# Six changed orders and three split sums of squares in a two-block layer kernel on one core

## The reference

```python
# block 1
h = rmsnorm(x, norm1_g)
u_a, u_b, u_c, u_d, u_g = split(h @ w_in)
branches = [short_conv(u_a), stick_breaking_attention(u_b), mamba2(u_c), moba(u_d)]
merged = sum(sigmoid(u_g[i]) * (branches[i] @ w_branch[i]))
x = x + merged @ w_o
h2 = rmsnorm(x, norm2_g)
g_ff, up_ff = split(h2 @ w_gate_up)
x = x + (silu(g_ff) * up_ff) @ w_down
x = rmsnorm(x, final_g)
# block 2
h = rmsnorm(x, norm_g_2)
# windowed attention with sinks (q, k, v, za) and a gated token mixing (u, vs, zs)
y = ga * (attention @ w_att_out) + gs * (mixing @ w_sg_out)
out = rmsnorm(x + y @ w_o_2, final_g_2)
```

## Time and profile before

| | us |
|---|---|
| median of 3 runs | 1333.63 (1333.63 to 1334.12) |
| the profiled execution | 1333.23 |
| its span | 1331.20 |
| TensorE busy | 1321.4 |
| VectorE, ScalarE, GpSimd busy | 582.5, 509.6, 597.1 |
| mean granted TensorE clock | 0.998 of full speed |

### The profile page before, as it was taken

One profiled execution on the slowest core, in us unless ns is written; L12 is line 12 of the kernel. 1 busy time (PEld: TensorE's weight loads), 2 busy tenths in 40 slices (PEclk: granted clock), 3 DMA queues, 4 the chain that ended last, 5 costly groups with the idle time before them and its releaser, 6 DMA issues.

```text
span 1331.2 us, 16999 instructions
## 1 busy us (share of the span) xinstructions
PE 1321.4 (99%) x6518; PEld 1081.4 (81%) x6518; DVE 582.5 (44%) x947; ACT 509.6 (38%) x729; POOL 597.1 (45%) x448
## 2 busy tenths in 40 slices
PE   9999999999999999999999999999999999999998
PEld 8877777888888888888888887877777888888887
DVE  3674444556554433213322347766654322242333
ACT  6222534566433533222211236254655224342233
POOL 4453333443644364445554546433432553435441
PEclk9999999999999999999999999999999999999999
DMA  6333152413233343333333323322221332423321
GB/s 202 95 113 102 40 151 64 126 41 119 79 97 134 95 115 106 95 95 95 95 95 95 87 71 111 103 69 77 91 68 59 127 95 64 127 64 100 102 83 64
DMA packets 144493, 126.70 MB, mean 95 GB/s; under 512 B 4464, under 2 KB 139760, under 8 KB 144432
## 3 DMA queue, kind: packets, MB, share of 16 engines
q1 hardware_dynamic: 144080, 125.66, 30.7%
q10 hardware_dynamic: 352, 0.19, 0.1%
HBM read 120.46 MB, written 2.10 MB: 92 GB/s over the span
## 4 chain that ended last, share of the span: by engine, by line
PE 96%; DVE 2%; ACT 1%; issue 0%; DMA 0%; SPq 0%; ACTq 0%; DVEq 0%
PE gemm L592 25%; PE gemm L600 25%; PE gemm L593 25%; PE gemm L649 2%; PE gemm L650 2%; PE gemm L653 2%; PE gemm L616 2%; PE gemm L617 2%; PE gemm L622 2%; PE mix L978 1%; PE mix L966 1%; PE mix L955 1%; PE mix L1032 1%; PE mix L802 1%; PE gemm L677 1%; PE mix L827 0%
## 5 line engine op out<-in xcount | busy, mean ns | idle before, releaser
L525 POOL TENSOR_TENSOR wlo<-raw,whi 128x512 fp32r<-128x512 f32 x424 | 571.9, 1379 | 551.0 <-ACT whi L1130 551.0
L592 PE MATMUL gemm<-hh,whi 128*128 128x512 f32 x1128 | 444.9, 394 | 0.4 <-ACT whi L1130 0.4
L593 PE MATMUL gemm<-hl,whi 128*128 128x512 f32 x1128 | 439.6, 390 | 0.0
L600 PE MATMUL gemm<-hh,wlo 128*128 128x512 f32 x1128 | 280.3, 390 | 0.0
L1130 ACT ACTIVATE whi<-raw 128x2048 fp32r<-128x2048 f32 x106 | 202.5, 1911 | 193.4 <-PE gemm L600 164.6
L592 PEld LDWEIGHTS gemm<-hh,whi 128*128 128x128 f32 x1128 | 211.8, 188 | 49.2 <-issue 4.6
L593 PEld LDWEIGHTS gemm<-hl,whi 128*128 128x128 f32 x1128 | 212.0, 188 | 43.1 <-issue 0.5
L600 PEld LDWEIGHTS gemm<-hh,wlo 128*128 128x128 f32 x1128 | 211.4, 188 | 43.6
L521 POOL TENSOR_TENSOR wlo_b<-raw_b,whi_b 128x512 fp32r<-128x512 f32 x16 | 20.6, 1287 | 146.2 <-ACT whi L1130 146.2
L1850 DVE TENSOR_TENSOR fu_t<-gemm,R 128x512 f32<-128x512 f32 x22 | 15.2, 691 | 99.7 <-PE gemm L600 99.7
L592 PE MATMUL gemm<-ah,whi 128*128 128x512 f32 x132 | 51.5, 390 | 0.5 <-DVE xT L1829 0.5
(11 more groups left out here) (443 smaller groups left out, 1863.9 us busy)
## 6 DMA issues: line engine op xcount, KB each, us to landing
raw<-w_in SPq DMA_DIRECT2D x53, 1024.0 KB, 5.3
raw<-w_gu SPq DMA_DIRECT2D x44, 512.0 KB, 4.7
raw<-w_o SPq DMA_DIRECT2D x8, 1024.0 KB, 5.1
raw<-w_down SPq DMA_DIRECT2D x16, 512.0 KB, 4.0
raw_b<-w_branch SPq DMA_DIRECT2D x16, 256.0 KB, 5.6
raw<-w_ao SPq DMA_DIRECT2D x4, 1024.0 KB, 5.1
raw<-w_so SPq DMA_DIRECT2D x4, 1024.0 KB, 5.0
raw<-w_in SPq DMA_DIRECT2D x7, 512.0 KB, 4.6
```

Source lines behind the costliest of these rows:

```text
L525: last = nc.gpsimd.tensor_tensor(a(wlo), a(raw), as_f32(a(whi)), ALU.subtract)
L592: mm(bank[:, :], w, xh[:, k, :], start=(k == 0), stop=False)
L593: mm(bank[:, :], w, xl[:, k, :], start=False, stop=False)
L600: last = mm(bank[:, :], wlo_[:, s, k, col:col + P], xh[:, k, :], start=False, stop=(k == kts - 1))
```

## The change

Six orders and three sums:

1. In `first_tile`, the 11 fill products behind `turn_in(0)` and `turn_in(1)` become 4, then `turn_in(2)` and `turn_in(3)`, then 5.
2. The sums over partitions of acc0, acc1 and acc2 are no longer one f32 product each. VectorE copies the accumulator to fp32r and subtracts the copy from it; TensorE adds two fp32r products with ones_r. `sum_rows` moves behind the second tile's products of unit 32; `sum_both` moves from unit 66 into the first tile of unit 67, behind ten products.
3. In units 62 to 65, ScalarE's split of the next unit stands between hh and the squares of an odd m instead of ahead of the next hh, and VectorE adds the squares of tile m - 1 in step m (those of 5 and 6 in step 6).
4. `turn_rows` moves into the second tile of unit 67, behind ten products.
5. The split of unit 81 moves ahead of the wait for `ln_var`.
6. `turn_out(0)` moves into unit 104, behind eight products. A seventh, small order on VectorE swaps `finish_q` and a `w_slot` in the attention.

```diff
--- before.py
+++ after.py
@@ -108,6 +108,7 @@
         hh = place("hh", [P, KD, SEQ], 76, f32r)
         hl = place("hl", [P, KD, SEQ], 92, f32r)
         c1 = place("c1", [P, 640], 108)
+        ones_r = place("ones_r", [P, P], 110.5, f32r)
         prm = place("prm", [P, NPAR], 112)
         sml = place("sml", [P, 256], 113)
         R = place("R", [P, SEQ], 114)
@@ -157,6 +158,8 @@
 
         acc0 = place("acc0", [P, SEQ], Z0)
         sq0 = place("sq0", [P, 2, SEQ], Z0 + 2)
+        acc0h = place("acc0h", [P, SEQ], Z0 + 6, f32r)
+        acc0l = place("acc0l", [P, SEQ], Z0 + 8, f32r)
 
         ah = place("ah", [P, 8, SEQ], Z0, f32r)
         al = place("al", [P, 8, SEQ], Z0 + 16, f32r)
@@ -164,6 +167,8 @@
         fu_t = place("fu_t", [P, 2, SEQ], Z0 + 68)
         acc1 = place("acc1", [P, SEQ], Z0 + 32)
         acc2 = place("acc2", [P, SEQ], Z0 + 34)
+        acch = place("acch", [P, 2, SEQ], Z0 + 48, f32r)
+        accl = place("accl", [P, 2, SEQ], Z0 + 52, f32r)
         sq1 = place("sq1", [P, 2, SEQ], Z0 + 36)
         sq2 = place("sq2", [P, 2, SEQ], Z0 + 40)
         r1 = place("r1", [P, SEQ], Z0 + 44)
@@ -681,9 +686,12 @@
                 pe.wait_ge(sem("ident_in"), 16)
                 for m in range(2):
                     turn_in(m)
-                idle_products(11)
+                idle_products(4)
+                for m in range(2, 4):
+                    turn_in(m)
+                idle_products(5)
                 for k in range(KD):
-                    if k in (0, 2, 4):
+                    if k in (2, 4):
                         turn_in(k + 2)
                         turn_in(k + 3)
                     if k in (0, 4):
@@ -889,9 +897,11 @@
             for f, (n0, part, h0) in enumerate(ffn_units):
                 if f == 0:
                     def sum_rows():
-                        pe.wait_ge(sem("acc0"), KD)
-                        mm(M[0][:, :], ones, acc0[:, :], start=True, stop=True).then_inc(sem("norm_ps"), 1)
-                    unit_last_k(n0, hh, hl, KD, ("h_lo", KD), sum_rows)
+                        pe.wait_ge(sem("ones_r"), 1)
+                        pe.wait_ge(sem("acc0_lo"), 2)
+                        mm(M[0][:, :], ones_r[:, :], acc0h[:, :], start=True, stop=False)
+                        mm(M[0][:, :], ones_r[:, :], acc0l[:, :], start=False, stop=True).then_inc(sem("norm_ps"), 1)
+                    unit_last_k(n0, hh, hl, KD, ("h_lo", KD), sum_rows, 1)
                     unit_fm(n0 + 1)
                 with pe.Fori(1 if f == 0 else 0, part // 2) as i:
                     for s in range(2):
@@ -905,10 +915,12 @@
 
 
             def sum_both():
-                pe.wait_ge(sem("acc2"), KD)
-                mm(M[0][:, :], ones, acc1[:, :], start=True, stop=True)
-                mm(M[1][:, :], ones, acc2[:, :], start=True, stop=True).then_inc(sem("norm_ps"), 1)
-            unit_last_k(n_e0, hh, hl, KD, ("h_lo", 2 * KD), sum_both, 1)
+                pe.wait_ge(sem("acc_lo"), 3)
+                for i in range(2):
+                    mm(M[i][:, :], ones_r[:, :], acch[:, i, :], start=True, stop=False)
+                    last = mm(M[i][:, :], ones_r[:, :], accl[:, i, :], start=False, stop=True)
+                last.then_inc(sem("norm_ps"), 1)
+            unit_last_k(n_e0, hh, hl, KD, ("h_lo", 2 * KD))
 
             def turn_rows():
 
@@ -998,9 +1010,9 @@
                 for u in range(2):
                     for j in range(2):
                         gemm_fm(tiles_before(n + u) + j, n + u, (n + u) % 2, hh, hl, KD, j * P, j == 0,
-                                hooks={at: w_slot for at in W_AT[2 * u + j]} if p else None)
-                        if p == 0 and u == 0:
-                            (turn_rows, turn_keys)[j]()
+                                hooks={at: w_slot for at in W_AT[2 * u + j]} if p else {10: (sum_both, turn_rows)[j]} if u == 0 else None)
+                        if p == 0 and u == 0 and j == 1:
+                            turn_keys()
             for p in range(4):
                 n = n_vs + p
                 wide_unit(n, p % 2, tiles_before(n - p % 2), lambda t: w_slot())
@@ -1089,9 +1101,9 @@
                 last.then_inc(sem("norm_ps"), 1)
 
             unit_last_k(n_o2, y2h, y2l, KD, ("y2_lo", 0))
-            turn_out(0)
             for p in range(1, 3):
-                unit_fm(n_o2 + p, y2h, y2l, after=lambda j: turn_out(2 * p + j - 1))
+                unit_fm(n_o2 + p, y2h, y2l, after=lambda j: turn_out(2 * p + j - 1),
+                        hooks={8: lambda: turn_out(0)} if p == 1 else None)
             last_tile(6, 0)
             turn_out(5)
             last_tile(7, 0)
@@ -1330,14 +1342,15 @@
                         for j in range(2):
                             split(n0 + part + j + 1, i)
                     continue
+                split(n0 + part + 1)
                 for m in range(KD):
                     n = n0 + part + m // 2
-                    if m % 2 == 0:
-                        split(n + 1)
                     act.wait_ge(sem("tile_free"), tiles_before(n) + m % 2 + 1)
                     if m >= 2:
                         act.wait_ge(sem("acc2"), m - 1)
                     fn(hh[:, m, :], xT[:, m, :], ACT.Copy, scale=fgng[:, m:m + 1]).then_inc(sem("h_hi"), 1)
+                    if m % 2 and m < KD - 1:
+                        split(n + 2)
                     fn(sq1[:, m % 2, :], xT[:, m, :], ACT.Square)
                     fn(sq2[:, m % 2, :], xT[:, m, :], ACT.Square, scale=pcol("fg", m)).then_inc(sem("sq12"), 1)
             split(n_e0 + 1)
@@ -1434,13 +1447,14 @@
             for t in range(TT):
                 act.wait_ge(sem("tile_free"), tiles_before(n_vs + 4))
                 fn(vg[:, t, :], vg[:, t, :], ACT.Gelu).then_inc(sem("vs_act"), 1)
+            split(n_ga + 2)
             act.wait_ge(sem("ln_var"), 1)
             fn(lrs, lrs, ACT.Sqrt).then_inc(sem("ln_rs"), 1)
 
             def gates(n0, buf, i0, bias0):
                 for p in range(4):
                     for u in range(2):
-                        if n0 != n_ga or p + u > 0:
+                        if n0 != n_ga or p > 0:
                             split(n0 + 2 * p + u + 1)
                         if u == 0:
                             for j in range(2):
@@ -1566,6 +1580,8 @@
 
             dve.wait_ge(sem("r_ps"), 1)
             link(v.tensor_copy(R[:, :], M[0][:, :]))
+            dve.wait_ge(sem("c1_in"), 16)
+            v.tensor_copy(ones_r[:, :], ones).then_inc(sem("ones_r"), 1)
             v.memset(cbuf[:, :, 0:2], 0.0)
             link(v.memset(xbuf[:, :, 0:3], 0.0))
             link(v.memset(wdt[:, :, :], 0.0))
@@ -1835,6 +1851,10 @@
                     op0=ALU.mult, op1=ALU.subtract).then_inc(sem("h_lo"), 1)
                 dve.wait_ge(sem("sq0"), m + 1)
                 accumulate(acc0, sq0, m, "acc0")
+            dve.wait_ge(sem("acc0"), KD)
+            v.tensor_copy(acc0h[:, :], acc0[:, :]).then_inc(sem("acc0_lo"), 1)
+            dve.wait_ge(sem("acc0_lo"), 1)
+            tt(acc0l[:, :], acc0[:, :], as_f32(acc0h[:, :]), ALU.subtract).then_inc(sem("acc0_lo"), 1)
             dve.wait_ge(sem("R2"), 1)
 
 
@@ -1874,12 +1894,19 @@
                     dve.wait_ge(sem("h_hi"), 2 * KD + m + 1)
                     stt(out=hl[:, m, :], in0=xT[:, m, :], scalar=fgng[:, m:m + 1], in1=as_f32(hh[:, m, :]),
                         op0=ALU.mult, op1=ALU.subtract).then_inc(sem("h_lo"), 1)
-                    dve.wait_ge(sem("sq12"), m + 1)
-                    accumulate(acc1, sq1, m, "acc1")
-                    accumulate(acc2, sq2, m, "acc2")
+                    for done in {0: (), KD - 2: (m - 1, m), KD - 1: (m,)}.get(m, (m - 1,)):
+                        dve.wait_ge(sem("sq12"), done + 1)
+                        accumulate(acc1, sq1, done, "acc1")
+                        accumulate(acc2, sq2, done, "acc2")
 
 
             dve.wait_ge(sem("acc1"), KD)
+            v.tensor_copy(acch[:, 0, :], acc1[:, :])
+            dve.wait_ge(sem("acc2"), KD)
+            v.tensor_copy(acch[:, 1, :], acc2[:, :]).then_inc(sem("acc_lo"), 1)
+            dve.wait_ge(sem("acc_lo"), 1)
+            for i, a in enumerate((acc1, acc2)):
+                tt(accl[:, i, :], a[:, :], as_f32(acch[:, i, :]), ALU.subtract).then_inc(sem("acc_lo"), 1)
             v.memset(key_t[:, :, :], 0.0)
             link(v.memset(rope_t[:, :, :], 0.0))
             dve.wait_ge(sem("rms12"), 1)
@@ -2034,8 +2061,8 @@
                 w_slot()
                 w_slot(lambda: take_q(1))
                 gate_attention(p - 1)
+                w_slot()
                 finish_q()
-                w_slot()
                 take_za(0)
                 w_slot(lambda: scale_x(0))
                 w_slot()
```

## The result

The changed kernel takes 1337.53 us (median of 7 runs, 1337.07 to 1340.04); the kernel before, run beside it, 1333.56 (1333.23 to 1334.12). The ratio is 1.0034 [1.0024, 1.0043]: slower by 4.0 us by the medians and 4.5 by the ratio, where 2.9 was forecast. One execution of the kernel before, among those timed beside the experiments, took 1652.40 us at a granted clock of 0.752, a slow state that is no property of the kernel; ratios and spreads leave it out, and the median of 1333.43 in two rows of the table of experiments would be 1333.29 without it. The profiled execution of the changed kernel took 1339.0 (span 1337.0), the longest kind; its stages are compared with those of the profiled execution before (1333.23, span 1331.2).

A forecast was written before the change was run, and what follows sets the result against it. The prediction took TensorE, busy 99% of the span, as the bound. Its terms, -0.45 + 3.15 + 1.7 - 0.7 - 0.8 = +2.9, gave 1336.1 us on 1333.23, 1336.5 against the median; range 1334.3 to 1338.0.

The forecast's parts named there:

- Rival D: Start gives nothing and second-block entry costs its upper bound, hl of tile 6 being late: +3.95, 1337.6 us; chance 0.12.
- Start, gates, output: First real product, unit 81 and turn_out(0): earlier starts or removed waits gain 0.45, 0.7 and 0.8 us.
- Feed-forward entry: At unit 33: late sum_rows delays the norm and whi behind it on ScalarE, a loss of 3.15 us.
- Rival A: Entries at units 33 and 68: whi not behind the norms, late sums hidden; sum -3.9, 1329.8 us; chance 0.08.
- the table load directly ahead of whi's Copy: ScalarE before unit 33: the row was trusted over the skill page's rule, which would make the loss 1.28 us smaller.
- Second-block entry: Units 67 and 68: unit 67 gains two to three us, then late sum_both delays whi; unit 68 starts 1.7 later.
- rival B: Unit 67's subtractions on VectorE not blocked by GpSimd: second entry +0.4, sum +1.6, 1335.2 us; chance 0.20.
- The claim that turn_rows and turn_keys cost nothing: Inside unit 67: whatever they wait for is covered by the later wait in front of unit 68; no extra cost.
- the price of a wait: Ahead of unit 33: 3.07 us lost, made 3.15 because the first product after a wait takes 0.50, others 0.39.

The follow-up runs named there:

- four orders alone: Kernel before with only the start, the attention swap of finish_q and w_slot, unit 81's split and turn_out(0) changed: 1330.84 us, ratio 0.9982.
- late sum alone: Kernel before with only sum_rows moved behind unit 32's second tile, still as an f32 product: 1338.31 us, ratio 1.0038.
- new steps alone: Kernel before with only the new order in units 62 to 65, the f32 sums in unit 66 as before: 1333.10 us, ratio 0.9999.

## Why the prediction was right or wrong

**Right in direction and in where the time is lost, short in the sum.** Slower was the likeliest side, and 1337.53 lies inside the range; by the ratio on the median shown, 1338.2, it is 0.2 above its end. Against the forecast of 1336.5 the change is 1.0 to 1.7 slower. That the median came so near is in part luck: it is of the shorter kind of execution, and the execution whose stages are known took 1339.0, 1.0 above the end of the range. Rival D's 1337.6 is near for no reason of its own: the start did give its 0.45, and the second entry stayed inside the forecast's bounds.

**Start, gates, output**: -0.45 (the 3.25 us that became 2.80), -0.7, -0.8, as forecast. The four orders alone confirmed them together with the swap in the attention.

**Feed-forward entry**: unit 33 was forecast 2.6 later, without the clock, and is 2.59 later. Its cause is shown from two sides, by the sum early and by whi early; both remove all of it. Rival A, that whi does not stand behind the norm, is refuted by the trace of the change (Ln, Exp, table load and whi end to end) and by whi's early order: only there does the late sum cost nothing. One reading was wrong without changing the forecast: the prediction took the table load directly ahead of whi's Copy as a sign that this Copy can need one. In the kernel with unit 33's whi ahead of the norm two such Copies run without it, one behind a Square (456.38) and one behind the Silu (467.69). So the load ahead of the Copy, 1.28 of what held unit 33 back, comes from where the load was placed; no run changed that alone.

**Second-block entry**: unit 68 was put 1.7 later; it is 1.9 later. The first part was right: unit 67 was put at 825.7 to 827.0 on the forecast's own time, that is two to three us gained, and its start of 830.70 less the 4.3 by which everything runs late there (3.1 + 1.7 - 0.5) is 826.4, within it. In the same way Ln was put at 830.4 to 831.6, and 835.45 less 4.3 is 831.2. The subtractions are blocked (3.37; the forecast 3.3), so rival B fell; where GpSimd waits for them and they take 1.30, unit 68 comes 1.2 earlier by the edit, and rival B's difference was 1.3. The claim that turn_rows and turn_keys cost nothing held for the change (0.25 at turn_keys), but not where whi of unit 68 is freed: then GpSimd holds up VectorE by 2.0 and turn_keys stands 1.96. This is in part why freeing both whi gives 1332.2 and not the 1329.8 of rival A; such a time came only with the sums themselves early (1329.31).

**The step that failed** is the price of a wait in the sum: its length and "the first product after a wait takes 0.50 where others take 0.39", in the terms 3.15 and 1.7. The waits themselves were sized right (3.1 and 1.9). What the sum put at nothing, without a reason, is what comes behind them: the granted clock falls to the 1.2 GHz level for 6 to 13 products. In the trace of the change this is 1.7 behind unit 33's wait and 1.6 behind unit 68's, 3.3 in all, and 2.8 behind the one wait of the late sum alone. In medians, the change less the kernel with unit 33's whi first is 6.0, of which the wait is 3.6: 2.4 is left for the slow products of both stretches. Behind the start, the longest break in TensorE's line before was 0.97 (ahead of unit 66), so the trace never showed what a break of three us brings; the range was made of waits only and had no room for it.

**A term left out**: the swap of finish_q and w_slot was told among the orders and not costed. In the attention, before, there is a wait of 0.4 for att_t (L1962) which is not in the list of waits after: -0.4. It is gone in the kernel with the four orders alone too, and still there with the new steps alone; no run has the swap by itself. This term and the clock's pull opposite ways: +2.9 + 3.3 - 0.4 is 5.8, and the span grew by 5.8.

**Open**: why a wait of 1.86 ahead of unit 68 is followed by slow products in the three traces that had a wait for whi at both places (the change twice, and GpSimd waiting), and not in the two that had the second alone; nor was the 1.96 at turn_keys followed by any, in the kernel that kept the wait at unit 33. The traces show the connection and not what makes it. Open too is in which of the two stretches the shorter executions (1336.6 to 1337.5) save their 2 us: no trace caught one. Taking the copies and subtractions away but leaving the sum late in unit 67 wasn't tried.

## What to carry to other kernels

When a reduction is moved later because its own engine has room there, follow the one who waits for it: here two cheap products, 4.4 us later, held back a norm, and ScalarE's order had the next weights behind that norm. Either leave the reduction early, at the price of dearer products, or first take the work that others wait for out from behind the norm. Look also at whom the work that comes earlier holds up: here GpSimd's wlo held up VectorE and took 2 us back. And where one engine runs without a break, price a new wait of some us above its length: here a wait of 3.5 us cost 5.1 alone, and one of 3.6 cost 6.0 in the change, with the second slow stretch that came along.

## What the runs showed of the hardware

- A single wait of 3.5 us at unit 33, in a line of products that had run for hundreds of us at 2.4 GHz, was followed by 6 to 13 products at 1.2 GHz (0.43 apart, 0.63 long) in each of the five traces that had it (the change twice, late sum alone, unit 68's whi early, GpSimd waiting); in the seven traces without it (before among them) no such stretch is to be found. A wait of 1.9 alone was followed by none.
- Kernels without that wait spread over at most 1.4 us (before: 1332.78 to 1334.16 in 27 runs), those with it over 1.6 to 3.0.
- The place of a Copy in ScalarE's order changed how many table loads there are. With unit 33's whi ahead of the norm and the first loop step written out, ScalarE has 722 instructions, not 729, and 9.0 us less busy time: seven loads of 1.28. It gave no time that can be seen: the kernel with sum_rows early has 729 instructions and takes 1332.24, this one 1332.06.
- Blocking between VectorE and GpSimd goes both ways: GpSimd's four operations on wlo took 5.93 beside the two subtractions and 5.06 when they had ended, while VectorE's pair took 3.37 and 1.30. With GpSimd busy throughout, the R of 0.69 took 1.84.
